# Stick-breaking attention: the absolute value moves from ScalarE to VectorE and ahead of the present unit's softplus

## The reference, cut to what matters

```python
z = jnp.einsum('bhqd,bhkd->bhqk', qb, k).astype(jnp.float32) * scale
log_keep = jnp.where(valid, jax.nn.log_sigmoid(-z), 0.0)
log_tail = lax.cumsum(log_keep, axis=3, reverse=True) - log_keep
w = jnp.where(valid, jnp.exp(jax.nn.log_sigmoid(z) + log_tail), 0.0)
return jnp.einsum('bhqk,bhkd->bhqd', w.astype(v.dtype), v)
```

## Time and profile before

| what | value |
|---|---|
| median of 3 runs | 3872.57 us (3871.29 to 3883.3) |
| the profiled execution | 3879.3 us, of which the span is 3877.2 us |
| mean granted TensorE clock | 0.99 of full speed |
| PE busy | 3658.1 us (94%) |
| PEld busy | 2805.9 us (72%) |
| DVE busy | 1570.4 us (41%) |
| ACT busy | 1153.2 us (30%) |
| POOL busy | 1000.0 us (26%) |

### The profile page before, as it was taken

How to read it: one execution, slowest core, us unless ns; L and a number is a source line. 1 busy time by engine, 2 the same in 40 slices (tenths; PEclk the granted TensorE clock), 3 DMA queues, 4 the chain that set the end, 5 groups by cost and what they waited for, 6 DMA issues and landing times. The chain is left out here.

```text
span 3877.2 us, 69380 instructions
## 1 busy us (share of the span) xinstructions
PE 3658.1 (94%) x29776; PEld 2805.9 (72%) x29776; DVE 1570.4 (41%) x3002; ACT 1153.2 (30%) x2210; POOL 1000.0 (26%) x1668
## 2 busy tenths in 40 slices
PE   6899999998999999999889999999999999999998
PEld 5664667986646679879767777776787468888886
DVE  6635545345355444521764444444003242212123
ACT  2436333014363331201644444443110121101011
POOL 4120005231200051332022222221422033434442
PEclk9999999999999999999999999999999999999999
DMA  4131202211211012212110010001222211111112
GB/s 157 45 98 41 66 13 65 89 66 66 77 52 55 23 55 99 110 44 77 50 38 19 26 31 25 25 25 35 74 80 71 87 44 55 44 45 54 44 66 98
DMA packets 190201, 225.90 MB, mean 58 GB/s; under 512 B 20990, under 2 KB 168000, under 8 KB 187080
## 3 DMA queue, kind: packets, MB, share of 16 engines
q1 hardware_dynamic: 189896, 221.47, 17.4%
HBM read 188.89 MB, written 32.56 MB: 57 GB/s over the span
## 5 line engine op out<-in xcount | busy, mean ns | idle before, releaser
L200 POOL CAST weights_high<-weights_value 128x256 fp32r<-128x256 f32 x272 | 113.7, 466 | 1119.6 <-DMA weights_value<-in_w_in_dram 932.5
L218 PE MATMUL banks<-h_high,weights_high 128*128 128x512 f32 x608 | 238.7, 393 | 8.0 <-PEq L852 5.9
L4081 POOL CAST ffn_weights_high<-ffn_weights_value 128x256 fp32r<-128x256 f32 x256 | 103.7, 454 | 530.8 <-DMA ffn_weights_value<-in_w_ff_dram 344.7
L218 PE MATMUL banks<-h_high,weights_low 128*128 128x512 f32 x608 | 236.9, 390 | 0.0
L204 POOL TENSOR_TENSOR weights_low<-weights_value,weights_high 128x256 fp32r<-128x256 f32 x272 | 217.2, 834 | 2.7
L218 PE MATMUL banks<-ffn_in_high,ffn_weights_high 128*128 128x512 f32 x512 | 200.7, 392 | 6.7 <-POOL ffn_weights_low L4085 3.2
L218 PE MATMUL banks<-ffn_in_low,ffn_weights_high 128*128 128x512 f32 x512 | 200.1, 391 | 0.0
L218 PE MATMUL banks<-ffn_in_high,ffn_weights_low 128*128 128x512 f32 x512 | 200.0, 391 | 0.0
L218 PE MATMUL banks<-ffn_weights_high,hidden_high 128*128 128x512 f32 x512 | 199.4, 390 | 0.0
L218 PE MATMUL banks<-ffn_weights_low,hidden_high 128*128 128x512 f32 x512 | 199.4, 389 | 0.0
L218 PE MATMUL banks<-ffn_weights_high,hidden_low 128*128 128x512 f32 x512 | 199.4, 389 | 0.0
(11 more groups left out here) (486 smaller groups left out, 9154.1 us busy)
## 6 DMA issues: line engine op xcount, KB each, us to landing
ffn_weights_value<-in_w_ff_dram SPq DMA_DIRECT2D x32, 1024.0 KB, 5.3
weights_value<-in_w_in_dram SPq DMA_DIRECT2D x24, 1024.0 KB, 5.4
attention_scratch<-in_ada_w_dram SPq DMA_DIRECT2D x12, 1024.0 KB, 5.2
pair_weights_value<-in_w_in_dram SPq DMA_DIRECT2D x24, 512.0 KB, 4.1
ndow_weights_value<-in_w_in_dram SPq DMA_DIRECT2D x10, 1024.0 KB, 5.2
weights_value<-in_w_out_dram SPq DMA_DIRECT2D x8, 1024.0 KB, 5.8
gates_value<-in_w_in_dram SPq DMA_DIRECT2D x16, 512.0 KB, 5.4
first_mixed<-in_ada_w_dram SPq DMA_DIRECT2D x6, 1024.0 KB, 6.1
```

The costliest lines, as they stand in the source:

```text
L200: last = nc.gpsimd.tensor_copy(high[:, i, :], value[:, i, :])
L218: mm = nc.tensor.matmul(out, x, y, start=(first and i == 0 and j == 0), stop=(last and i == n - 1 and j == 2))
L4081: last = nc.gpsimd.tensor_copy(high[:, i], value[:, i])
```

## The change

ScalarE's `ACT.Abs` and its two waits go. VectorE gets a new step `absolute(u)`, which reads the scores from PSUM as 32-bit integers, clears the top bit and writes to `z_bufs`. It waits for the scores of unit `u` and, from unit 2 on, for the softplus of unit `u-2`, whose buffer it overwrites. VectorE's program takes the absolute values of units 0 and 1 first of all, and from round 1 on that of unit `it+1` at the head of round `it`, in front of the softplus of unit `it`.

```diff
             def softplus_log(u):
                 x = part(z_bufs, u)
-                act.wait_ge(scores_done, u + 1)
-                if u >= 2:
-                    act.wait_ge(softplus_ready, u - 1)
-                nc.scalar.activation(x, z(u), ACT.Abs).then_inc(abs_ready, 1)
                 act.wait_ge(abs_ready, u + 1)
                 nc.scalar.activation(x, x, ACT.Exp, scale=-1.0).then_inc(exp_ready, 1)
...
         @block.vector
         def _(dve):
+            def absolute(u):
+                dve.wait_ge(scores_done, u + 1)
+                if u >= 2:
+                    dve.wait_ge(softplus_ready, u - 1)
+                nc.vector.tensor_scalar(part(z_bufs, u).bitcast(I32), z(u).bitcast(I32), 0x7FFFFFFF, None, ALU.bitwise_and).then_inc(abs_ready, 1)
+
...
+            absolute(0)
             for it in range(N + 2):
                 if it == 0:
+                    absolute(1)
                     value_moves(0)
+                elif it + 1 < N:
+                    absolute(it + 1)
                 if it < N:
                     softplus(it)
```

## The result

The changed kernel takes 3994.74 us (median of 4 runs, 3984.53 to 4018.33), the kernel before beside it 3877.94 (median of 4, 3871.29 to 3884.7). The ratio is 1.0311, 95% interval 1.0282 to 1.0341: slower by 3.1%. Forecast were 3993 us, 3948 to 4040. The profiled execution took 3996.4 us with a span of 3993.5.

A forecast was written before the change was run, and what follows sets the result against it. It took TensorE, busy 94% of the span, to bound the kernel, with 12.05 us standing in a stage. Gaps of 81 us plus 39 for the clock gave +120, so 3999, less 6.7: 3993 us, range 3948 to 4040.

The forecast's parts named there:

- The wait in front of the softplus: VectorE stands for the next unit's scores with the present softplus queued behind; TensorE gaps sum to 50.3 us a stage.
- The stage without the clock's part: Length of a stick-breaking stage with the gaps but at full clock: 142.2 us instead of 101.6.
- The term for two stages: Growth of both stick-breaking stages from the gaps alone, without the clock: +81 us.
- The price of the absolute value: Time of VectorE's absolute value with input in PSUM, taken as 1.22 us for 128x1024.
- The lower bound from SBUF: Rival: the absolute value on VectorE costs 0.83 us, a third less; kernel about 3970 us, chance 0.09.
- The clock: TensorE's gaps bring falls to 1.2 GHz, 12 a stage at 1.7 us each: +39 us net.
- ScalarE's relief: Absolute values leave ScalarE, shortening the chain from scores to softplus: at most 9.65 us a stage.
- ScalarE waiting in front of the exponent: Sign expected in the changed kernel's profile: ScalarE's waits now stand in front of the exponent; no size given.
- The rival that the clock holds: TensorE's clock stays up in both stages and only the wait is paid: 3954 us, chance 0.14.
- The rival on the other side: The wait costs nothing and ScalarE's relief counts, stages of 92 us: 3853 us, chance 0.03.

The follow-up runs named there:

- e4: The changed kernel with TensorE multiplying the identity with itself in the gaps before the tails, all waits kept: 3953.28 us, ratio 1.02.
- e1: The changed kernel with the next unit's absolute value directly behind the present unit's softplus instead of ahead of it: 3883.84 us, ratio 1.0026.
- e3: The changed kernel with every absolute value taken twice, one behind the other, at the same place: 4069.4 us, ratio 1.0508.
- e5: The changed kernel with the scores of the next unit a round earlier on TensorE: 3867.55 us, ratio 0.9974.
- e2: The kernel before with the absolute value left out altogether, so it computes another function: 3866.22 us, ratio 0.9973.
- e8: The kernel before with scores a round earlier and the softplus as log(1 + exp(z)) on ScalarE, valid while exp(z) is finite: 3860.82 us, ratio 0.9955.
- e6: The kernel before with the scores a round earlier on TensorE, the absolute value still on ScalarE: 3866.89 us, ratio 0.997.

## Why the prediction was right

**The wait in front of the softplus** was the step that decided, and its numbers hold. Forecast were gaps of 2.54 us and 2.99 on the diagonal; rounds 8 and 9 show 2.51 and 2.98. Forecast were 50.3 us over units 1 to 22; the trace has 49.7 us, of which 0.55 are the wait of unit 23, which the prediction counted apart at 0.8. The stage without the clock's part was to take 142.2 us; e4 took 141.7. The term for two stages, 81 us, measures 2 x 40.1 = 80. e1, e3 and e5 show the mechanism from three sides: swap the two, and it goes; double the absolute value, and the gap grows by all of it; bring the scores earlier, and it goes.

**The price of the absolute value**, 1.22 us for 128x1024, taken from VectorE's TENSOR_SCALAR with its input in PSUM, is 1.22 to 1.23. The lower bound from SBUF, 0.83, had no part in it.

**The clock** was the right mechanism, its size somewhat high. Forecast were 39 us net. Measured are 7.9 + 26.0, less the 1.2 us by which the second stage before was longer than the first, so 32.7. The forecast had 12 falls in each stage, 3.4 us each. Read off in windows of 0.2 us, the changed kernel's first stage has 5 falls, all of 3.4 us, and the second has 12, of which four are longer (6.8 to 10.8 us). One of the short falls and two of the long ones, the last of which goes on past the end of the stage:

```profile
309.30:312.70 3.40, 3.06 (x4) 1.18 (x4) 1.57 (x3) 1.30 (x2) 0.00 (x0) 0.50 0.02 5
1125.10:1135.30 10.20, 7.74 (x16) 2.21 (x14) 3.64 (x4) 3.55 (x5) 0.00 (x0) 0.50 0.00 1
1241.10:1251.90 10.80, 8.16 (x40) 4.76 (x40) 5.79 (x16) 2.81 (x8) 0.00 (x0) 0.50 0.00 0
```

So there were 17 falls instead of 24, and each cost 1.6 us in the first stage (7.9 / 5) and 2.2 in the second (26.0 / 12) instead of 1.7. The count was too high and the price a little too low, and the two errors partly cancel. The stages have the same instructions and still lost 8 and 26 us: how often a gap of 2 to 3 us brings a fall isn't the same from pass to pass, as the split of rows 10, three of seven, had shown. That also spreads the runs: the slowest of the four, 4018.33 us, has a mean clock of 0.972, the fastest, 3984.53, one of 0.982. The forecast's size was within what these rows can give, its hit to 2 us was luck in part. The stages give 80 + 33 = 113 us of the forecast 120, about 4 more came from the rest of the program, which the change doesn't touch, and the kernel before measured beside the changed one took 5.4 us more than the 3872.57 that the forecast was added to. Of the difference itself 120 us were forecast and 117 measured.

**ScalarE's relief** was bounded at 9.65 us a stage, and e2 gave 7.4. In the changed kernel none of it shows, as argued: ScalarE now waits in front of exp for the absolute value (2.64 us ahead of the exp of unit 10):

```profile
324.20 1.06 ACT L715 ACTIVATE attention_scratch<-attention_scratch 128x1024 f32<-128x1024 f32 x1 [2.64 <-DVE attention_scratch L747]
```

The prediction had ScalarE waiting in front of the exponent; it waits there too, 32.1 + 17.3 us in the first stage, but 38.6 in front of exp as well. This is off the path and changed no term.

```profile
ACT attention_scratch L715 <- DVE attention_scratch L747: 38.6, 22, 2.6
ACT attention_scratch L725 <- DVE banks L765: 32.1, 13, 9.4
ACT attention_scratch L725 <- PE banks L668: 17.3, 9, 3.2
```

**The rival that the clock holds** gave 3954 us, and e4, which makes it hold, gave 3953.28. The rival on the other side, 3853 us for stages of 92 us, was not where this change could go, but its floor was real: e8 has stages of 91.9 and 91.5 us and 3860.82 us.

## What to carry to other kernels

On an engine that takes its instructions in order, work for the next unit placed at the head of a round is work ahead only if its input is ready there; otherwise it puts that input's wait in front of everything of the present unit. Look up, in the program of the engine that produces the input, what stands right behind it: if that is the consumer of what you now queue behind the wait, the two operations that lay side by side become a sum in each round. Where the input can be made a round earlier (here the scores, with a free pair of banks), that is the edit to make first. Here it gave 5.6 us in the first stage (e6, 101.6 - 96.0) with the absolute value left on ScalarE, where leaving it out altogether gave 7.4 (e2).

## What the runs showed of the hardware

- Gaps on TensorE that come back every round, here 23 in a stage and the longest 3.0 us, can cost more than themselves. In the changed kernel's stages the clock averaged 0.94 and 0.80, in e3 with gaps up to 4.2 us 0.81 and 0.78; multiplying the identity into a bank that is free at that time, for most of each gap, kept it at 1.00 and gave back 34 us in the two stages (e4).
- Outside the stages the program is the same in all kernels. In the profiled executions it took from 3399.8 us (e2, 663.0 + 2736.8) to 3417.6 (e8, 666.3 + 2751.3), with 3406.1 before and 3410.0 in the changed kernel. The two rows of e8 show the clock a hundredth lower over the long part, and TensorE 15.7 us longer busy there than before (2639.35 against 2623.66) with as many records:

```profile
359.10:1025.40 666.30, 629.68 (x4252) 510.66 (x4252) 303.87 (x699) 191.06 (x449) 153.93 (x272) 0.99 0.21 69
1116.90:3868.20 2751.30, 2639.35 (x23308) 2057.41 (x23308) 1002.56 (x1778) 718.71 (x1371) 749.67 (x1232) 0.98 0.17 55
```

This spread of 18 us is as large as what e2 and e5 to e8 gain, so the windows of the stages tell them apart better than the medians do.
